# The first layer's modulation vector: scale half as a row of fp32 products on TensorE, shift half on VectorE

## The reference, cut to what matters

```python
def adaln_params(c, w, b):                      # c (1, 1024), w (1024, 3072)
    mod = jax.nn.silu(c) @ w + b
    shift, scale, gate = jnp.split(mod, 3, axis=-1)
    ...
for i in range(DEPTH):
    shift, scale, gate = adaln_params(c, ada_w[i], ada_b[i])
    h = rms_norm(x, norm_g[i]) * (1.0 + scale) + shift
    branch = attention_branch(h, ...) if i % 2 == 0 else pool_branch(h, ...)
    x = x + gate * branch
```

## Time and profile before

| | |
|---|---|
| time, median of 3 runs | 1502.27 us (1500.41 to 1504.61) |
| profiled execution, its own time | 1505.06 us |
| its span, first to last instruction | 1503.3 us |
| TensorE busy | 1427.0 us, 95% of the span |
| VectorE busy | 883.5 us, 59% |
| ScalarE, GpSimd busy | 529.0 us, 405.4 us |

### The profile page before, as it was taken

One profiled execution on the slowest core, in us unless ns is written; L12 is line 12 of the kernel. 1 busy time (PEld: TensorE's weight loads), 2 busy tenths in 40 slices (PEclk: granted clock), 3 DMA queues, 4 the chain that ended last, 5 costly groups with the idle time before them and its releaser, 6 DMA issues.

```text
span 1503.3 us, 20206 instructions
## 1 busy us (share of the span) xinstructions
PE 1427.0 (95%) x7240; PEld 1206.8 (80%) x7240; DVE 883.5 (59%) x1524; ACT 529.0 (35%) x1270; POOL 405.4 (27%) x551
## 2 busy tenths in 40 slices
PE   1799999999999998899999999899999999999999
PEld 1578887788778887788898998788888888888887
DVE  7777666765444449887677675535555443555522
ACT  2544433433211118765555553322213122221200
POOL 2333333322122215655556555310000100000000
PEclk9999999999999999999999999999999999999999
DMA  8645555534988788757767666831121552112142
GB/s 304 229 171 191 195 194 194 191 122 155 342 333 319 271 328 307 257 210 283 264 258 284 255 225 232 283 98 43 42 77 52 180 184 75 43 42 77 50 154 84
DMA packets 96787, 285.62 MB, mean 190 GB/s; under 512 B 10768, under 2 KB 40496, under 8 KB 87088
## 3 DMA queue, kind: packets, MB, share of 16 engines
q1 hardware_dynamic: 87760, 250.74, 46.4%
q0 software_dynamic: 8928, 33.59, 6.5%
HBM read 196.22 MB, written 88.08 MB: 189 GB/s over the span
## 4 chain that ended last, share of the span: by engine, by line
PE 72%; DMA 9%; DVE 6%; issue 5%; POOL 3%; ACT 3%; SPq 1%; POOLq 0%; DVEq 0%; ACTq 0%
PE po_f_ps L1845 23%; PE po_y_ps L1861 12%; PE at_y_ps L1415 9%; PE ga_g_ps L929 9%; PE qk_proj L663 7%; PE at_o_ps L1399 5%; PE at_s_ps L1371 3%; DMA values_split<-qk_late 3%; DMA po_xn<-x_mid_t 2%; POOL at_pt L1143 2%; DMA ga_ada<-in_ada_w 2%; PE at_tr L1381 1%; DMA ga_raw<-in_attn_w_gate 1%; POOL qk_rq L306 1%; DMA qk_raw<-in_attn_w_qkv 1%
## 5 line engine op out<-in xcount | busy, mean ns | idle before, releaser
L1845 PE MATMUL po_f_ps<-po_ht,po_w 128*128 128x512 f32 x1536 | 348.9, 389 | 0.0
L1845 PEld LDWEIGHTS po_f_ps<-po_ht,po_w 128*128 128x128 f32 x1536 | 288.2, 188 | 60.0 <-DVE po_ht L1707 0.3
L663 PE MATMUL qk_proj<-qk_w_qkv,qk_ht 128*128 128x512 f32 x1152 | 280.0, 398 | 8.1 <-DVE qk_ht L458 4.1
L663 PEld LDWEIGHTS qk_proj<-qk_w_qkv,qk_ht 128*128 128x128 f32 x1152 | 214.6, 190 | 55.1 <-issue 5.9
L1415 PE MATMUL at_y_ps<-at_zt,at_w 128*128 128x512 f32 x768 | 197.1, 398 | 4.3 <-DVE at_x L1304 4.3
L1861 PE MATMUL po_y_ps<-po_zt,po_w 128*128 128x512 f32 x768 | 174.7, 389 | 0.0
L1861 PEld LDWEIGHTS po_y_ps<-po_zt,po_w 128*128 128x128 f32 x768 | 144.1, 188 | 29.9
L1415 PEld LDWEIGHTS at_y_ps<-at_zt,at_w 128*128 128x128 f32 x768 | 137.4, 189 | 29.3 <-issue 5.5
L1143 POOL TENSOR_SCALAR_AFFINE_SELECT at_pt<-at_ph 128x512 fp32r<-128x512 f32 x128 | 96.6, 776 | 141.9 <-ACT at_ph L1198 141.9
L1694 DVE TENSOR_TENSOR po_w<-po_raw,po_w 128x1024 fp32r<-128x1024 f32 x48 | 58.8, 1225 | 128.0 <-ACT po_w L1628 128.0
L306 POOL TENSOR_TENSOR qk_rq<-qk_mq,qk_half 128x8 f32<-128x8 f32 (+1 forms) x48 | 70.2, 1463 | 177.4 <-DVE qk_mq L485 177.3
(11 more groups left out here) (168 smaller groups left out, 1971.2 us busy)
## 6 DMA issues: line engine op xcount, KB each, us to landing
at_w<-out_weight_split SPq DMA_DIRECT2D x32, 1024.0 KB, 7.3
queries_t<-qk_late SPq DMA_DIRECT2D x16, 1024.0 KB, 4.3
ga_ada<-in_ada_w POOLq DMA_DIRECT2D x64, 256.0 KB, 5.3
at_qt<-queries_t SPq DMA_DIRECT2D x16, 1024.0 KB, 8.6
ht_split<-qk_ht SPq DMA_DIRECT2D x6, 2048.0 KB, 9.6
values_split<-qk_late SPq DMA_DIRECT2D x16, 768.0 KB, 4.5
at_vs<-values_split SPq DMA_DIRECT2D x16, 768.0 KB, 4.9
qk_late<-in_ada_w SPq DMA_DIRECT2D x16, 512.0 KB, 6.1
```

Source lines behind the costliest of these rows:

```text
L663: last = nc.tensor.matmul(proj[:, b * BANK:(b + 1) * BANK], ht[:, s % 2, m, k, t * P:(t + 1) * P], w_qkv[:, w, k, b * BANK:(b + 1) * BANK] ...
L1845: last = nc.tensor.matmul(f_ps[:, bank(j, h), :], w[:, i % 2, a, k, :], ht[:, h, m, k, :], start=(n == 0), stop=(n == 3 * KC - 1))
```

## The change

The pieces are now ordered so that even ones (0, 2, ...) are the shift half and odd ones the scale half of the same chunk of c. VectorE sums the even ones as before. For an odd piece TensorE does two matmuls in plain fp32: stationary is the one column of silu(c), moving the 512 columns of half a piece, accumulated over the 8 chunks into one partition of proj (row_ps, 1 x 1024 in two banks). Piece i is free when its own engine is done with it (ada_used). When all 8 are in, ScalarE copies the row to SBUF in two halves (row, act_ready), and TensorE turns it to columns by 8 matmuls with a 1 x 128 stationary and a single one moving. All three parts of the columns, and spread behind them, now stand behind the products in TensorE's order; sum_squares stands behind the sixth. The four small loads are issued by GpSimd behind its memsets, not by SyncE. reduce_angle stands behind VectorE's second and fourth sum, mean_x behind the seventh. VectorE's splits of items 0 to 2 move behind set_scale, and each of w_low(0) to w_low(3) stands ahead of a pair of modulated chunks.

```diff
     proj, tr, st_ps, bc_ps = (ps[n] for n in ("proj", "tr", "st_ps", "bc_ps"))
+    row_ps, row = proj[0:1, 0:D], sums[0:1, D:2 * D]
 
...
     q_stored, k_stored, v_stored = sem("q_stored"), sem("k_stored"), sem("v_stored")
-    consts_set, act_begun, silu_done, vec = sem("consts_set"), sem("act_begun"), sem("silu_done"), sem("vec")
+    consts_set, act_ready, silu_done, vec = sem("consts_set"), sem("act_ready"), sem("silu_done"), sem("vec")
     trig_arg, pre_done = sem("trig_arg"), sem("pre_done")
...
 
+    def ada_used(i):
+        return (ada_added, mod_summed)[i % 2], i // 2 + 1
+
     MOD_PARTS = ((0, KC), (KC, KC + KC // 2), (KC + KC // 2, MODC))
...
             if i in BORROWED:
-                sp.wait_ge(ada_added, ADA - AS + i - RAW + 1)
+                sp.wait_ge(*ada_used(ADA - AS + i - RAW))
             elif i >= RAW:
...
         for i in range(ADA):
-            wait(sp, ada_added, i - AS + 1)
-            sp.dma_start(ada[:, i % AS, :], ada_v[i % KC][:, i // KC * SPAN:(i // KC + 1) * SPAN]).then_inc(ada_loaded[i % AS], 16)
+            if i >= AS:
+                sp.wait_ge(*ada_used(i - AS))
+            sp.dma_start(ada[:, i % AS, :], ada_v[i // 2][:, i % 2 * SPAN:(i % 2 + 1) * SPAN]).then_inc(ada_loaded[i % AS], 16)
             if i == AS - 1:
                 load_x(0)
-                sp.dma_start(bias[:, :], ada_b[0]).then_inc(small_loaded, 16)
-                sp.dma_start(g_col[:, :], norm_g[0]).then_inc(small_loaded, 16)
-                sp.dma_start(gq[:, :], q_norm[0].partition_broadcast(P)).then_inc(small_loaded, 16)
-                sp.dma_start(gk[:, :], k_norm[0].partition_broadcast(P)).then_inc(small_loaded, 16)
         for i in range(ITEMS):
...
         nc.gpsimd.memset(ones[:, :], 1.0).then_inc(consts_set, 1)
+        pool.dma_start(bias[:, :], ada_b[0]).then_inc(small_loaded, 16)
+        pool.dma_start(g_col[:, :], norm_g[0]).then_inc(small_loaded, 16)
+        pool.dma_start(gq[:, :], q_norm[0].partition_broadcast(P)).then_inc(small_loaded, 16)
+        pool.dma_start(gk[:, :], k_norm[0].partition_broadcast(P)).then_inc(small_loaded, 16)
         pool.wait_ge(consts_set, 4)
...
         rstd_x(0)
-        pool.wait_ge(mod_summed, len(MOD_PARTS))
+        pool.wait_ge(mod_summed, KC + len(MOD_PARTS))
         nc.gpsimd.memset(vs, 0.0).then_inc(consts_set, 1)
...
         act.wait_ge(c_loaded, 32)
-        nc.scalar.activation(c_tanh[:, :], c_col[:, :], ACT.Tanh, scale=0.5).then_inc(act_begun, 1)
+        nc.scalar.activation(c_tanh[:, :], c_col[:, :], ACT.Tanh, scale=0.5).then_inc(act_ready, 1)
         square_x(0, range(KC))
         act.wait_ge(trig_arg, 1)
-        nc.scalar.activation(sin[:, :, HALF:ROT], red, ACT.Sin).then_inc(act_begun, 1)
+        nc.scalar.activation(sin[:, :, HALF:ROT], red, ACT.Sin).then_inc(act_ready, 1)
         act.wait_ge(trig_arg, 2)
-        nc.scalar.activation(cos[:, :, 0:HALF], red2, ACT.Sin).then_inc(act_begun, 1)
+        nc.scalar.activation(cos[:, :, 0:HALF], red2, ACT.Sin).then_inc(act_ready, 1)
+        act.wait_ge(mod_summed, KC)
+        for h in range(2):
+            nc.scalar.activation(row[:, h * BANK:(h + 1) * BANK], row_ps[:, h * BANK:(h + 1) * BANK], ACT.Copy).then_inc(act_ready, 1)
         for i in range(RAW):
...
         def add_ada(i):
-            k, part = i % KC, sums[:, i // KC * SPAN:(i // KC + 1) * SPAN]
+            k, part = i // 2, sums[:, 0:D]
             dve.wait_ge(ada_loaded[i % AS], 16 * (i // AS + 1))
...
             else:
-                dve.wait_ge(ada_added, i)
+                dve.wait_ge(ada_added, k)
                 nc.vector.scalar_tensor_tensor(part, ada[:, i % AS, :], c_silu[:, k:k + 1], part, ALU.mult, ALU.add).then_inc(ada_added, 1)
...
             cols = slice(*MOD_PARTS[part])
-            dve.wait_ge(mod_summed, part + 1)
+            dve.wait_ge(mod_summed, KC + part + 1)
             nc.vector.tensor_tensor(mod[:, cols], tr[:, part, 0:KC // 2], bias[:, cols], ALU.add).then_inc(pre_done, 1)
...
 
-        dve.wait_ge(act_begun, 1)
+        dve.wait_ge(act_ready, 1)
         nc.vector.scalar_tensor_tensor(c_twice[:, :], c_tanh[:, :], 1.0, c_col[:, :], ALU.add,
...
             link(nc.vector.tensor_scalar(ang[:, :, f], pos_f[:, :], float(inv_freq[f]), None, ALU.mult))
-        for i in range(ADA):
-            add_ada(i)
-            if i == 4:
+        for k in range(KC):
+            add_ada(2 * k)
+            if k == 1:
                 reduce_angle(0.0, red)
-            if i == 9:
+            if k == 3:
                 reduce_angle(0.25, red2)
-            if i == ADA - 7:
+            if k == KC - 2:
                 mean_x(0)
         dve.wait_ge(small_loaded, 64)
-        dve.wait_ge(act_begun, 3)
+        dve.wait_ge(act_ready, 3)
         nc.vector.tensor_copy(cos[:, :, HALF:ROT], cos[:, :, 0:HALF]).then_inc(pre_done, 1)
...
         dve.wait_ge(pre_done, 4)
-        for i in range(RAW):
-            w_low(i)
-        dve.wait_ge(mod_summed, 1)
+        dve.wait_ge(mod_summed, KC + 1)
         nc.vector.tensor_tensor(mod[:, 0:KC], tr[:, 0, 0:KC], bias[:, 0:KC], ALU.add).then_inc(pre_done, 1)
         set_scale(1)
-        modulate(0, range(KC // 2))
         set_scale(2)
-        w_low(RAW)
-        modulate(0, range(KC // 2, KC))
+        for i in range(KC // KP):
+            w_low(i)
+            modulate(0, range(KP * i, KP * (i + 1)))
         for i in range(RAW + 1, RAW + AS + 3):
...
         pe.wait_ge(consts_set, 4)
+        pe.wait_ge(silu_done, 2)
+        for k in range(KC):
+            i = 2 * k + 1
+            pe.wait_ge(ada_loaded[i % AS], 16 * (i // AS + 1))
+            for h in range(2):
+                last = nc.tensor.matmul(row_ps[:, h * BANK:(h + 1) * BANK], c_silu[:, k:k + 1], ada[:, i % AS, h * BANK:(h + 1) * BANK],
+                                        start=(k == 0), stop=(k == KC - 1))
+            last.then_inc(mod_summed, 1)
+            if k == KC - 3:
+                sum_squares(pe, 0)
         for part, (first, end) in enumerate(MOD_PARTS):
-            pe.wait_ge(ada_added, KC if part == 0 else ADA)
+            if part == 0:
+                pe.wait_ge(ada_added, KC)
+            else:
+                pe.wait_ge(act_ready, 3 + part)
             for j in range(first, end):
-                last = nc.tensor.matmul(tr[:, part, j - first:j - first + 1], sums[:, j * P:(j + 1) * P], ones[:, :], start=True, stop=True)
+                if part == 0:
+                    last = nc.tensor.matmul(tr[:, part, j - first:j - first + 1], sums[:, j * P:(j + 1) * P], ones[:, :], start=True, stop=True)
+                else:
+                    last = nc.tensor.matmul(tr[:, part, j - first:j - first + 1], row[:, (j - KC) * P:(j - KC + 1) * P], ones[0:1, :],
+                                            start=True, stop=True)
             last.then_inc(mod_summed, 1)
-            if part == 0:
-                sum_squares(pe, 0)
-                spread(pe, 0)
+        spread(pe, 0)
         for n in range(NB):
...
```

## The result

The changed kernel takes 1509.87 us (median of 6, 1505.81 to 1513.64) against 1503.28 of the kernel before (6 runs): ratio 1.0054, 95% interval 1.0035 to 1.0073. The kernel is slower by 0.4 to 0.5%, beyond the 0.3% (4.5 us) that the prediction counted as no change. The forecast of no change (1502.1) was wrong, and the range (to 1509.8) missed the time by a hair; the price is near that of rival (a), its mechanism isn't.

What follows compares the result with a forecast made beforehand. Matmuls bound the kernel (TensorE 95% busy), shifted by VectorE's opening chain. 3.6 us won ahead of the modulation and 3.6 given back by uncovered splits left 1505.0 profiled, 1502.1 in the median's frame; range 1498.5 to 1509.8.

Steps and rivals of the forecast that it cites:

- rival (a): TensorE's clock never rises on one stationary column, 3.4 us a piece: 6.3 us slower, 1508.6; chance 0.37.
- The stream of pieces: Loads of the modulation weights: x at 13.65, 1.0 us for small loads, 11 pieces of 1.40; last lands at 30.1.
- the hole of 3.1 us: Slow DMA stretch from 13.7 to 16.8 in the kernel before, at the small loads; 1.0 us of it kept.
- The prediction's own sign: Test on the stream: if the sixth piece lands later than 16.5, the hole is not gone.
- The rule on turns: DMA engines alternate queues by packet, so small loads no longer block a piece; only their engine time is left.
- The ring's bound: Five load slots: 5.3 us issue to landing plus 1.7 us use, 7.0 us for 5 pieces, 1.40 each.
- Rival (c): The ring, fed back by the slower of two engines, stalls loads: last piece 2 us later, 1504; chance 0.08.
- The last piece's product: TensorE's matmuls on the last piece: landing at 30.1, plus 0.1 and 1.8 us, used at 32.0.
- flickers at worst: Claim that TensorE's clock comes up on the first pieces and then at most flickers.
- The clock: TensorE's disputed term in the opening: a piece costs 1.8 us at full clock, 3.4 at half; taken to rise.
- The columns: TensorE's 32 instructions behind the last product: 7.0 us at half clock, 4.5 at full, 5.5 taken, ending at 37.5.
- the loop: VectorE's four splits and chunk pairs: 13.1 us, ending at 51.0; uncovered splits give back 3.6 us.

Runs made afterwards that it cites:

- e12: Changed kernel with the four small loads back on SyncE's queue behind x, a repeat for a trace; ratio to the kernel before 1.0020.
- e11: Changed kernel with VectorE's second reduce_angle moved from behind the fourth sum to behind the sixth; 1506.1 us, ratio 1.0017 to the kernel before.
- e9: Kernel before with gq and gk loaded behind the eleventh weight item and scaled behind split 10; 1499.75 us, ratio 0.9978 to the kernel before.
- e4: Changed kernel with filling matmuls ahead of the first product and behind each of the first seven; ratio 1.0035 to the kernel before.
- e7: Changed kernel with TensorE's products of chunks 1 to 6 cut to 128 of 512 columns per half; 1512.24 us, ratio 1.0064 to the kernel before.
- e5: Changed kernel run again without edits, to see the spread; 1509.17 us, ratio 1.0044 to the kernel before.
- e3: Changed kernel with VectorE's splits 0 to 2 ahead of its wait for the columns and ScalarE's high parts ahead of the row copies; ratio 1.0044 to before.
- e13: Changed kernel with only VectorE's splits 0 to 2 ahead of its wait for the columns; 1507.2 us, ratio 1.0035 to the kernel before.
- e2: Kernel before with only the four small loads moved to GpSimd's queue; ratio 1.0005 to the kernel before.
- e8: Changed kernel with small loads behind the third raw item, splits and high parts 0 to 2 early, second reduce_angle behind the sixth sum; 1503.37 us, ratio 1.0004 to before.
- e10: Changed kernel with gq and gk loaded late, splits 0 to 2 early, copies between high parts 0 and 1, second reduce_angle later; 1498.94 us, ratio 0.9974 to before.

## Why the prediction was wrong

- **The stream of pieces** is the step that failed: the last landing was put at 30.1 and came at 34.9. "I keep 1.0 us of the hole of 3.1 us": x landed at 17.39, 2.7 us behind the 14.65 of the sum and 3.7 behind before. That 1.0 came from the 44% busy share of the earlier trace rows, taken as the small loads' engine time. But the share holds the pieces' packets too, and it is of SyncE's queue; on GpSimd's the same 80 KB took 2.5 us of all engines' time in 3.6 us. On SyncE's queue the hole is as long with the engines less than half busy (0.44 before, 0.38 in e12), and what holds the stream there is open. The prediction's own sign spoke at once: the sixth piece landed at 18.67, later than 16.5.
- **The rule on turns.** By the Trainium skill ("DMA: Bandwidth & Descriptors", "Queues, rings and completion order") an engine takes turns among its queues by packets, and the prediction read from it that the pieces are spared. The trace agrees with the turns, as packets of both queues moved in the same 3.6 us (45 and 129), and not with the reading: the third piece landed 3.0 us late. Turns by packets spare nobody when the other queue's packets take five times as long.
- **What the late x set off.** It was not followed further: x late, additions late, angles beside the additions, the sum of piece 8 and its slot late. From x to the last piece it took 17.5 us in place of 15.4, and that is the other 2.1 of the 4.8 us. e11 (the angles moved) and e12 (x earlier) each got back about 3 us of time.
- **The ring's bound.** "5.3 us from issue to landing in an empty queue" misreads its row: the piece issued at 25.22 landed only at 31.28, 2.15 us after the last one was issued. In e9 the last piece took 3.6 us (26.93 to 30.56). Its term, 1.40 a piece, stood 0.06 over that of the transfers alone, so little came of it.
- **Whether the ring gives back.** Rival (c) named it, 8% at 2 us, and blamed the slower of two engines. It was VectorE, not TensorE: e4 left the landing where it was with TensorE at full clock, e7 with a quarter of its middle work, and piece 13 was issued at the end of VectorE's sum of piece 8 in the changed kernel's, e4's and e7's traces alike.
- **The last piece's product** is the second term that was off: 1.9 us from its landing forecast, 4.0 measured, since the last two products ran mostly at half clock. The forecast's "flickers at worst" was right in kind and had no price in the sum; it cost 2.1 us in one trace and 0.7 in e5.
- **The clock.** Rival (a) (it never rises on one column) is refuted: it rose between 9.9 and 12.7 us in most traces, within or just behind the first products, and the price at full clock was 1.88 us (1.8 forecast), 3.57 at half (3.4). When it rises isn't fixed, though: in e3 and e11 the second product took 3.57 us as well, and the clock came up only near 22 us. The Trainium skill ("TensorE: Matmul & The Clock Gate", "HAM oscillation — how this bites in real kernels") warned of just this shape, short bursts with waits for transfers between. Here the trace agrees: the falls at 17.9 and 31.5 us came within waits of 3.7 and 2.5 us. By that rule the prediction had put the time between the forecast (1502.1) and (a) (1508.6); it came out above both.
- **Luck.** That the time came near that of (a), 1508.6, is chance: (a) has the last product end at 36.0 and low clock on every piece; here the stream was late and the clock mostly up.
- **The columns** (5.5 forecast, 4.5 to 7.0 its ends; measured 4.5, 3.8 in e5, 7.1 in e7) and **the loop** (13.1; 13.4) were right. That splits without cover give back 3.6 us is right for the loop (3.4 in e3 and e13); in time no run shows it. The lower end of the range, 1498.5, isn't reached by the sum's own terms (2.1 less is 1500.0).
- **Open: how the opening carries to the end.** In the profiled pair it is 6.4 us at the marker, 4.1 at the last matmul of the projection (line 663 there, 669 here: 366.3 and 370.4) and 5.4 at the end. In e5 it is 3.15, 1.1 (367.4) and 4.1. So e5's other 3 us come behind the projection, nearly all in attend_stage: its first score matmul (line 1371, here 1392) is 0.9 us late. From that matmul to the last of at_y_ps the stage takes 411.7 us before, 412.4 changed and 415.0 in e5, but also 412.6 in e2 and 414.5 in e9, which are the kernel before with loads moved: single traces differ by 3 us there, with or without the change. The clock's later falls don't explain it: behind 100 us it is low for 17 us before, 13.6 changed, 17 in e5. The medians are 6.6 and 6.7 us apart, more than any of these, and no run tells where the rest is; e8 shows that edits in the opening alone bring it all back.

## What to carry to other kernels

Before taking work off an engine in a stream, ask what feeds and what frees the stream's slots: here small loads and an unrelated VectorE call set the last landing. With them out of the way both divisions of the sums gained the same, so the gain was that of the loads, and halving VectorE's sums bought nothing that a time shows. A load of a few KB can hold the stream for 3 us, in which about a megabyte would pass at 390 GB/s (an estimate): place it by when it is used, not by its size. A busy share of the DMA engines is no price: the same loads showed 0.38 and 1.04 for holes of about the same length. And a matmul phase that waits for transfers pays for its clock behind the last piece; less work in it can be slower (e7).

## What the runs showed of the hardware

- Four loads of 80 KB in all held the stream at 122 to 138 GB/s for 3 to 3.6 us from GpSimd's queue, with a DMA share of 1.04 and 1.05, and at 140 and 168 GB/s for 3 us from SyncE's, with 0.38 (e12) and 0.44 (before). Of these gq and gk, one row read by 128 partitions, are nearly everything: without them x is followed by the sixth piece at 15.1 in place of 18.1 (e9), bias and g_col included.
- Under plain fp32 with a single stationary column the clock rose from 0.50 to 1.00, between 9.9 and 12.7 us in most traces (it streams from about 7.2 on) and only near 22 us in e3 and e11. It costs 0.43 us from start to start for 512 columns at full clock, 0.85 at half.
- A column made from a 1 x 128 stationary operand costs as much as from 128 x 128: 16 instructions took 1.94 and 1.95 us (e5, at full clock).
- VectorE's 128x128 instructions took up to 0.83 us beside GpSimd's additions, 0.22 to 0.29 apart from them (e11); the 128x1024 sums took 1.7 in place of 1.28 (e10).
